# Two one-hot buffers instead of three in the expert gate stage, and one value half-tile loaded earlier

## The reference, cut to what matters

```
act = gelu(einsum('tkd,td->tk', u_tab[e], h))   # 128 experts per token
out = einsum('tk,tkd->td', g * act, v_tab[e])   # g: softmax over each head's 16 picks
```

## Time and profile before

| | |
|---|---|
| median of 3 runs | 5078.1 us |
| lowest and highest run | 5073.5 and 5079.41 us |
| the profiled execution | 5073.5 us |
| its span | 5071.7 us |
| granted clock of PE, mean | 0.973 |
| PE busy | 4711.7 us (93%) |
| DVE busy | 2638.8 us (52%) |
| ACT busy | 519.1 us (10%) |
| POOL busy | 896.2 us (18%) |
| moved to and from memory | 1352.14 MB, mean 267 GB/s |

### The profile page before, as it was taken

One profiled execution on the slowest core, in us unless ns is written; L12 is line 12 of the kernel. 1 busy time (PEld: TensorE's weight loads), 2 busy tenths in 40 slices (PEclk: granted clock), 3 DMA queues, 4 the chain that ended last, 5 costly groups with the idle time before them and its releaser, 6 DMA issues.

```text
span 5071.7 us, 46738 instructions
## 1 busy us (share of the span) xinstructions
PE 4711.7 (93%) x18798; PEld 3413.2 (67%) x18798; DVE 2638.8 (52%) x4433; ACT 519.1 (10%) x1155; POOL 896.2 (18%) x691
## 2 busy tenths in 40 slices
PE   8999999999987888798998989999998779999998
PEld 7888888887655555565666768888877654444443
DVE  3444200047757575735555456666666795455520
ACT  1111100011010101010000011111000150000000
POOL 0000000000122212103333332111222202222200
PEclk9999999999999999999999999999999999999999
DMA  4433343544685868558889887668999919999974
GB/s 171 144 142 137 133 166 141 204 183 168 218 318 201 311 211 315 204 197 312 343 351 351 316 327 274 229 224 306 409 405 390 370 71 411 372 415 413 414 260 137
DMA packets 237849, 1352.14 MB, mean 267 GB/s; under 512 B 43185, under 2 KB 43441, under 8 KB 131138
## 3 DMA queue, kind: packets, MB, share of 16 engines
q1 hardware_dynamic: 143778, 665.97, 35.6%
q0 software_dynamic: 93856, 683.19, 34.3%
HBM read 1308.38 MB, written 40.16 MB: 266 GB/s over the span
## 4 chain that ended last, share of the span: by engine, by line
PE 61%; DMA 21%; DVE 13%; issue 3%; POOL 1%; ACT 1%; SPq 0%; POOLq 0%; DVEq 0%; ACTq 0%
PE ps L339 27%; DMA RING<-in_peer_u,idxA 9%; PE ps L636 8%; PE pm L636 8%; PE ps L614 8%; DMA RING<-in_peer_v,idxA 8%; DVE RING L811 3%; DVE BIG L1063 3%; DVE CUR L817 2%; PE ps L535 2%; PE ps L477 2%; DVE RA L1264 1%; DMA out<-BIG 1%; DMA RA<-in_peer_v 1%; POOL RING L1735 1%
## 5 line engine op out<-in xcount | busy, mean ns | idle before, releaser
L339 PE MATMUL ps<-X,BIG 128*128 128x320 f32 (+1 forms) x5632 | 1418.1, 414 | 34.9 <-DVE BIG L1163 34.2
L339 PEld LDWEIGHTS ps<-X,BIG 128*128 128x128 f32 x5632 | 1081.3, 193 | 355.9 <-issue 58.8
L811 DVE CUSTOM_DVE_ANT_0 RING<-RING,CUR 128x2048 f32<-128x2048 f32 x320 | 729.8, 2290 | 497.0 <-DMA RING<-in_peer_u,idxA 352.2
L817 DVE SCALAR_TENSOR_TENSOR CUR<-RING,wexp,CUR 128x2048 f32<-128x2048 f32 x320 | 752.4, 2351 | 430.5 <-DMA RING<-in_peer_v,idxA 321.7
L614 PE MATMUL ps<-X,RA 128*128 128x256 f32 x4096 | 898.4, 381 | 27.9 <-DVE BIG L1251 27.1
L614 PEld LDWEIGHTS ps<-X,RA 128*128 128x128 f32 x4096 | 775.9, 190 | 150.1 <-DVE BIG L1251 43.0
L1735 POOL DMA_INDIRECT RING<-in_peer_u,idxA x256 | 378.2, 1477 | 1503.7 <-DVE hidden L811 1152.2
L1735 POOL DMA_INDIRECT RING<-in_peer_v,idxA x256 | 357.4, 1396 | 961.1 <-DVE CUR L817 723.0
L636 PE MATMUL ps<-RA,BIG 128*128 128x512 f32 x1024 | 484.6, 596 | 11.4 <-DMA RA<-in_peer_v 10.5
L636 PE MATMUL pm<-RA,BIG 128*128 128x512 f32 x1024 | 481.2, 592 | 0.0
L636 PEld LDWEIGHTS ps<-RA,BIG 128*128 128x128 f32 x1024 | 192.6, 190 | 262.2 <-issue 212.0
(11 more groups left out here) (283 smaller groups left out, 2854.8 us busy)
## 6 DMA issues: line engine op xcount, KB each, us to landing
BIG<-in_w_in_b SPq DMA_DIRECT2D x64, 2048.0 KB, 9.0
RA<-in_uT SPq DMA_DIRECT2D x256, 512.0 KB
RA<-in_peer_v SPq DMA_DIRECT2D x256, 512.0 KB
BIG<-in_w_gb_b SPq DMA_DIRECT2D x16, 2048.0 KB, 8.1
BIG<-in_w_ga_b SPq DMA_DIRECT2D x16, 2048.0 KB, 8.3
BIG<-in_w_gla_o_b SPq DMA_DIRECT2D x16, 2048.0 KB, 10.4
BIG<-in_w_mix_b SPq DMA_DIRECT2D x16, 2048.0 KB, 10.7
BIG<-in_w_q_b SPq DMA_DIRECT2D x16, 2048.0 KB, 10.2
```

The source lines that it names most:

```text
L339: last = pe.matmul(bank[:, 0:n], w[:, k, j * P:(j + 1) * P], src[:, k, 0:n], start=(k == 0), stop=(k == kt - 1))
L811: row_used.on(dve.tensor_tensor_reduce(out=row, in0=row, in1=h2cur[0:n, :], scale=1.0, scalar=0.0, op0=ALU.mult, op1=ALU.add, accum_out=hi ...
L817: row_used.on(dve.scalar_tensor_tensor(out=cur[0:n, :], in0=row, scalar=wexp[0:n, par, k:k + 1], in1=cur[0:n, :], op0=ALU.mult, op1=ALU.ad ...
```

## The change

The ring of one-hot buffers has two buffers instead of three, at columns 2048 to 4095 of `RA`, so in slots 2 and 3 alone. DVE runs one step ahead instead of two: it makes the one-hots of q and then multiplies the gates of q - 1, where it multiplied those of q - 2. Slot 1 is thereby free during the gate stage, and half-tile 257 moves in front of SP's wait for that stage.

```diff
-        ohs = [part_of(RA, 1024 + 1024 * i, 2, 4, P) for i in range(3)]
+        ohs = [part_of(RA, 2048 + 1024 * i, 2, 4, P) for i in range(2)]
@@ PE, gate stage
-                    last = pe.matmul(bank[:, n * P:(n + 1) * P], ohs[q % 3][:, 1, n, :], ohs[q % 3][:, 0, n, :],
+                    last = pe.matmul(bank[:, n * P:(n + 1) * P], ohs[q % 2][:, 1, n, :], ohs[q % 2][:, 0, n, :],
@@ DVE, gate stage
             def onehots(q):
-                if q >= 3:
-                    dve.wait_ge(*ps_done.at("g", q - 3))
+                if q >= 2:
+                    dve.wait_ge(*ps_done.at("g", q - 2))
...
             onehots(0)
-            onehots(1)
-            for q in range(2, PT // 4):
+            for q in range(1, PT // 4):
                 onehots(q)
-                gate_hidden(q - 2)
-            gate_hidden(PT // 4 - 2)
+                gate_hidden(q - 1)
             gate_hidden(PT // 4 - 1)
@@ ACT, gate stage
-                    ins = fn(ohs[q % 3][:, 0, n, :], ohs[q % 3][:, 0, n, :], ACT.Copy,
+                    ins = fn(ohs[q % 2][:, 0, n, :], ohs[q % 2][:, 0, n, :], ACT.Copy,
@@ SP
-            for m in range(2 * NB + 1):
+            for m in range(2 * NB + 2):
                 uv_load(m)
             sp.wait_ge(*ps_done.at("g", PT // 4 - 1))
             sp.wait_ge(*gm_ready.at(PT // 4 - 1))
-            for m in range(2 * NB + 1, 4 * NB):
+            for m in range(2 * NB + 2, 4 * NB):
                 uv_load(m)
```

More of the change, by code:

```diff
@@ L1264, in onehots @@
                 onehot_ready.on(dve.tensor_tensor(
-                    ohs[q % 3], iota128[:, :].unsqueeze(1).unsqueeze(1).to_broadcast([P, 2, 4, P]),
+                    ohs[q % 2], iota128[:, :].unsqueeze(1).unsqueeze(1).to_broadcast([P, 2, 4, P]),
                     sel.unsqueeze(3).to_broadcast([P, 2, 4, P]), ALU.is_equal), q)
```

## The result

| | before | changed |
|---|---|---|
| median, 4 runs each | 5078.76 us | 5131.46 us |
| lowest and highest | 5073.5 and 5083.25 | 5126.0 and 5152.23 |
| ratio, 95% interval | | 1.0111 (1.0082 to 1.0141) |
| span of the profiled execution | 5071.7 us | 5144.1 us |
| gate stage, first one-hots to start of the last gates | 113.1 us | 169.8 us |

The medians lie 52.7 us apart (42 to 72 by the interval). I had forecast +29 and a time of 5105 in 5095 to 5118; the rival in which PE's clock falls stood there with 8% and 5132. The profiled execution of the changed kernel is 14 us slower than its median. Its 72.4 us of difference in span are +3.9 before the gate stage (which starts at 4050.2 instead of 4046.3), +56.7 in it, and +11.8 behind it.

The account below looks back on a forecast made before the run. DVE was taken to bound the gate stage; +28.9 (shorter lead), -0.5 (half-tile ahead) and +0.6 (moved load) gave +29.0 us, on a base of 5076 a forecast of 5105 us, range 5095 to 5118 at 83%.

Parts of the forecast that it names:

- What bounds the kernel: Gate stage: DVE is the bound at 1.733 us a step, and the stage's change moves the end one for one.
- The shorter lead, the main term: Gate stage: DVE waits for PE, two steps take 4.37 us, 2.185 each against 1.733; +28.9 us.
- the third part of the trip: Gate stage: from PE's start to the start of the gates on DVE, taken as 1.19 us.
- the trip: Gate stage: from DVE's one-hots through ACT and PE to the start of their gates, taken as 3.77 us.
- The sign that I had named for a fallen clock: Gate stage: a pitch above 2.5 us would show that PE's clock fell.
- The clock as a rival: Gate stage: PE's pauses lower its clock, two steps take 5.29 us, stage 56.5 us longer, about 5132; 8%.
- two stretches of 10 us: Evidence against a falling clock: PE busy for 5.18 and 4.70 us there with granted clock 1.00.
- The rival's arithmetic: Gate stage at PE's lower level: 31 x 5.29 - 31 x 3.467 = 56.5 us longer, plus the start.
- The half-tile ahead: Start of the v stage: PE's wait for half-tile 257 goes, -0.5 us, bounds -10.5 and +3.
- The load moved into the u stage: End of the u stage: half-tile 257 issued about 4018, in the gather chain's path; +0.6 us, between 0 and 1.25.
- Two buffers are enough: Gate stage: rival that DVE waits for nothing, stage stays at 1.733 us a step, 5076; 3%.
- its deciding point: Gate stage: for two buffers to suffice, one-hots to gates must take under 2.86 us; taken as 3.77.

Follow-up runs that it names:

- e1: Changed kernel with half-tile 257 loaded after the gate stage again, so only the two-buffer ring and new DVE order remain: 5134.22 us, ratio 1.0113.
- e2: Changed kernel with two more matmuls of 128 x 128, results unread, behind each step's four on PE: 5111.1 us, ratio 1.0060 against before.
- e4: Changed kernel with PE waiting for each scaled token by itself, not for all four: 5086.76 us against 5077.91 before, ratio 1.0016.
- e3: Kernel before, three buffers and old load, but DVE's changed order (gates of q - 1 behind one-hots of q): 5146.65 us, ratio 1.0138.
- e7: Changed kernel with one more matmul, result unread, behind each step's four on PE: 5117.65 us, ratio 1.0069 against before.
- e8: Kernel before with three buffers in X, four half-tiles loaded ahead, and POOL instead of DVE and ACT making the weighted one-hot side: 5178.34 us, ratio 1.0195.
- e9: Changed kernel with ACT taken out: DVE makes the weighted one-hot side itself in four instructions: 5112.85 us, ratio 1.0055 against before.
- e5: Kernel before (three buffers, old DVE order) with the first buffer in X and half-tile 257 loaded ahead: 5081.51 us against 5087.21, ratio 0.9993.
- e6: Kernel before with all three buffers in X and half-tiles 256 to 259 loaded ahead of the gate stage: 5081.02 us against 5087.21, ratio 0.9992.

## Why the prediction was wrong, point by point

- **What bounds the kernel.** Right: DVE's loop bounded the gate stage, and the stage passes its time on nearly one for one. In e1 (stage +56.5 us) the median moved 56.3, in e2 (+29.8) 33.2, in e4 (+9.3) 8.9; in e3 (+57.6) it was 68.7, with runs from 5124.71 to 5150.14. In e7 (+36.1), e8 (+97.6) and e9 (+30.6) it was 30.4, 91.1 and 26.0, 4.6 to 6.5 us less than the stage; in e5 and e6, whose stage is as before, the median also lies 6 us below before's.
- **The shorter lead, the main term.** The mechanism was right and its size was not. The step that failed is the third part of the trip, PE's start to the gates, taken at 1.19 us from the earlier trace rows, at the higher level. It measured 2.11 (4077.47, PE's start, to 4079.58, the gates) in all 55 steps of the stretch from 4074.82 on; only three whole groups ran in 1.16. With it the trip is 4.69 us, and two steps take 5.30. I had the 2.11 too, from the stage's start, and used it for the first gates only. The sign that I had named for a fallen clock, a pitch above 2.5, came. At the higher level the term is 29.8 (e2) for 28.9 forecast; with the clock it is 56.7.
- **The clock as a rival.** I gave it 8% on the ground of two stretches of 10 us with PE half busy at 1.00. They bear no such weight. The first, in the rows below this list, is dense work with one pause of 2.18 us ahead of it and one of 3.02 behind, and not a regular beat of short work and short pauses; the second holds one pause of 3.02 us, up to 2093.88, between two dense parts. The stage's own row was the nearest one: PE 63.38 of 95 at 1.00, from which the change takes a fifth away. By that row nothing was known of the clock below it, and an even chance would have been fair. The rival's arithmetic, 31 x (5.29 - 3.467), gave 56.5 for the 56.7 measured. The rule of the Trainium skill (TensorE: Matmul & The Clock Gate, section "A second HAM failure mode: psum-queue depth-cycling") that I had set aside, that short pauses between groups can move the clock, agrees with e7, which swings. It says that the clock swings; in the changed kernel itself it rose once and then stayed low for 145 us.
- **The half-tile ahead.** The wait went, as forecast (0.25 us of idling in the earlier trace rows, 0.4 by the starts, where I took 0.5), but PE entered the v stage at its lower level and lost 1.9 us. Nothing else came of the lead (e5, e6).
- **The load moved into the u stage.** Taken at 0.6 in 0 to 1.25. e1 against the changed kernel, and e5 and e6 against before, can't tell it from none.
- **Two buffers are enough.** Wrong for this kernel (e1), yet its deciding point held: with the trip shorter than the cover, DVE hardly waits (e9). There both sides moved, the trip without ACT and the cover with DVE's step of 2.2 us.
- **Left open.** The 11.8 us behind the gate stage in the profiled execution. PE's busy time grows by 7.3 us of them (884.08 to 891.33) and its waits for half-tiles by 4.0 (10.5 to 14.5). The longer busy time lies where the clock is low: at the stage's start (1.9), behind the 4.02 us wait, and for longer behind the 10.0 us wait (0.66 from 4321 to 4330, against 0.82 from 4257 to 4266 before). The nearest thing in another run is a wait of 3.40 us in e8, which has the longest v stage of the others (901.5); in e1, with the same order on DVE, it is 0.42 us and the v stage 897.1. In e5, with the same loads, none is over 0.98 but the long one. Why the wait of 4.02 came isn't shown; I take it for scatter, without proof.

PE in the kernel before, first and last row of the stretch 1835 to 1845 of the earlier trace rows, and the one after it:

```profile
1837.72 0.68 PE L407 MATMUL pm<-BIG 128*128 128x128 f32 x4 [2.18 <-issue]
...
1840.48 1.88 PE L415 MATMUL ps<-BIG 128*128 128x512 f32 x4
1845.38 0.82 PE L384 MATMUL pm<-RA 128*128 128x128 f32 x5 [3.02 <-DVE RA L935]
```

From 1837.72 on PE works without a pause to about 1842.4, and a mean over 10 us hid that.

## What to carry to other kernels

How many steps ahead an engine may work is set against the whole trip through the other engines, one step at a time: before a buffer is taken away, add up the trip at the bare latency and compare it with the work that stands between. Where the trip comes out longer, ask at once what the pauses do to PE's clock, and take PE's part of the trip at the lower level as well; a forecast at one level alone is half a forecast. And a signal for each quarter of the work can be worth nearly as much as a buffer: e4 gave back 47 of the 57 us that the third buffer with its lead was worth.

## What the runs showed that I had not expected

- PE can be busy for 114.01 of 145.00 us and still be held at 0.50. The lower level itself makes the busy time longer (2.08 for 1.16 us a step), so a high share doesn't say that PE is at full clock; the granted clock has to be read beside it.
- Useless work on PE made the changed kernel faster, though not as fast as before: two more matmuls a step took 26.9 us off the stage, and the median lies 23 us below that of e1 on the same chip.
- A `tensor_scalar` of 128 x 128 in f32 took 0.79 us on POOL, on DVE 0.34 in its record and about 0.26 from start to start (e9).
